# Expert matrices: who makes the first-key one-hot tables

## The chip, the cores and the metric

One Trainium2 chip; the kernel runs on one core of it. The metric is the device time of one execution in microseconds (us). The engines are named as in the profile: PE (TensorE matmuls), PEld (its weight loads), DVE (VectorE), ACT (ScalarE), POOL (GpSimd) and SP (SyncE, which here issues transfers). Each runs its own program in order and meets the others at counting semaphores.

## The reference, cut to what matters

One encoder layer for 1024 tokens of width 1024: token mixing, then a retrieval over 128 x 128 = 16,384 single-neuron experts. Each token has 8 heads; each head picks 16 experts, so a token has 128 picks, and an expert's number is a pair of keys (first, second):

```python
idx = first_key * PEER_KEYS + second_key      # PEER_KEYS = 128
g = softmax(best)                             # 16 weights per head
u = exp_u[idx]
a = gelu(einsum('td,ted->te', x, u)) * g
y = einsum('te,ted->td', a, exp_v[idx])
```

## The kernel before

The part that matters is `up_and_lists` (L1681 to L2181). It treats the eight blocks of 128 tokens in two ways. For the first four (ND = 4, numbered b = 0 to 3) it builds, for each token, a dense 128 x 128 matrix of expert weights, and stores these matrices in HBM (`route_scratch`); for the other four it only makes lists of expert numbers, and their experts' rows are gathered by indirect DMA.

A token's matrix is one matmul, `second` transposed times `first` (L2172). Both operands have one row per pick. A row of `first` is a one-hot of the pick's first key, times its weight; a row of `second` is a one-hot of its second key. They are made 8 tokens at a time (GROUP = 8; 16 groups, q = 0 to 15, to a block) in two slots, s = q % 2:
- DVE, L1993: eight `tensor_scalar` a group, one per token, which compare the key numbers with the token's first keys and multiply by the weights: 128 x 128 f32 each, two operands taken from one column (`key_pair`, `scaled`).
- ACT, L2091: eight activations a group, the distances |key number - second key|, written into `second`. ACT runs two groups ahead.
- DVE, L1999: one compare over the whole slot of `second` turns distances into ones and zeros, and raises `onehots`.
- PE: the eight matmuls, in two halves; each half raises `matrices`. Ahead of them in each group stands one unit (three matmuls) of another product, the up-projection of dense expert chunks (`piece`, L2127).
- ACT, L2109: copies each half out of PSUM into `stage` (`staged`). When a block is done, SP sends `stage` to HBM in 8 transfers of 1 MB (L1792), between loads of the next weights (`sc_u_raw`).

A slot may be written again when the matmuls of the group that used it are done (the waits on `matrices`, L1989 and L2088).

Between these, DVE's own queue holds other work, written out by hand in `tables` (L1979 to L2010). In blocks 0 and 1 each group is followed by one part of the top-16 selection of a later block (`routing`, L1866; parts 5 to 8 are its longest). In blocks 2 and 3 (DOT_BLOCKS) each group holds two dot products of a gathered expert row with the tokens (`pair_dot`, L2012), one ahead of the compare and one behind it. Their rows come through two buffers (`sc_eq` and `sc_prod`): POOL issues an indirect DMA for pick n (`fetch_pair`, L1832) once dot n - 2 has freed the buffer. Before the change POOL does nothing else in these blocks. One subtraction (`split_low`, L2027) follows groups 1 and 9. After the four blocks POOL fetches more rows into a ring of six (L1824), and DVE takes their dots (L2020).

Of the kernel before, what the change touches and what calls it, by code (L numbers as in the profile page):

```python
# [22 lines left out]
ALU = mybir.AluOpType  # L23
# [3 lines left out]
P = 128  # L27
# [18 lines left out]
WEIGHT_SCALE = 2.0 ** 14  # L46

ND = 4
# [11 lines left out]
class Layer:  # L60
# [1620 lines left out]
    def up_and_lists(self, vals, idxs, h2_hi, h2_lo, expert_at, expert_of, weight_of, dots):  # L1681
# [29 lines left out]
        listed = self.sem("sc_listed")  # L1711
        onehots = self.sem("sc_onehots")
        keys_ready = self.sem("sc_keys_ready")
        distances = self.sem("sc_distances")
        matrices = self.sem("sc_matrices")
        staged = self.sem("sc_staged")
# [31 lines left out]
        with ExitStack() as c:  # L1748
# [28 lines left out]
            with nc.Block() as block:  # L1777
# [40 lines left out]
                @block.gpsimd  # L1818
                def _(pool):
                    pool.iota(iota16[:], [[1, TOPK]], base=0, channel_multiplier=0, allow_small_or_imprecise_dtypes=True).then_inc(iotas, 1)  # L1820
                    pool.iota(key_of[:], [[1, KEYS]], base=0, channel_multiplier=0, allow_small_or_imprecise_dtypes=True).then_inc(iotas, 1)
                    every_u = self.u_rows.rearrange("i j d -> (i j) d")

                    def fetch_u(n):  # L1824
                        r = (n - GROUP_DOTS) % U_RING
                        if n >= GROUP_DOTS + U_RING:

                            pool.wait_ge(dotted, n - U_RING + 1)
                        pool.indirect_dma_start(u_rows[r], None, every_u,
                                                bass.IndirectOffsetOnAxis(ap=expert_at[:, n // P, n % P:n % P + 1], axis=0)).then_inc(u_got[r], 16)  # L1830

                    def fetch_pair(n):  # L1832
                        r = n % PAIR
                        if n >= PAIR:

                            pool.wait_ge(dotted, n - PAIR + 1)
                        pool.indirect_dma_start(pair_rows[r], None, every_u,
                                                bass.IndirectOffsetOnAxis(ap=expert_at[:, 0, n:n + 1], axis=0)).then_inc(pair_got[r], 16)
                    pool.wait_ge(listed, 1)
                    for i, b in enumerate(DOT_BLOCKS):  # L1840

                        pool.wait_ge(chosen, TURN_OF[b] + 1)
                        for n in range(i * BLOCK_DOTS, (i + 1) * BLOCK_DOTS):
                            fetch_pair(n)
                    pool.wait_ge(listed, BETWEEN)
                    pool.wait_ge(matrices, ND * QUADS)
                    for n in range(GROUP_DOTS, EARLY_DOTS):
                        if n == GROUP_DOTS + 2:

                            pool.wait_ge(stored, 16 * PIECES * ND)  # L1850
                        fetch_u(n)

                @block.vector
                def _(dve):
# [124 lines left out]
                    def tables(b):  # L1979
                        dve.wait_ge(turned, TURN_OF[b] + 1)  # L1980
                        dve.tensor_copy(key_pair[:].rearrange("k a t -> k (a t)"), ps[:, 4, 0:2 * P]).then_inc(keys_ready, 1)
                        do(dve.tensor_scalar(scaled[:], ps[:, 4, 2 * P:3 * P], WEIGHT_SCALE, None, ALU.mult))
                        all_so_far()
                        dve.wait_ge(keys_ready, b + 1)
                        for q in range(GROUPS):
                            s = q % 2
                            if b or q >= 2:

                                dve.wait_ge(matrices, b * QUADS + 2 * q - 2)  # L1989
                            for i in range(GROUP):  # L1990
                                t = q * GROUP + i
                                at_first = key_pair[:, 0, t:t + 1]
                                dve.tensor_scalar(first[:, s, i], key_of[:], at_first, scaled[:, t:t + 1], ALU.is_equal, ALU.mult)  # L1993

                            if b in DOT_BLOCKS:
                                at = DOT_BLOCKS.index(b) * BLOCK_DOTS + q * PER_GROUP
                                pair_dot(at)
                            dve.wait_ge(distances, b * GROUPS + q + 1)
                            dve.tensor_scalar(second[:, s].rearrange("k g n -> k (g n)"), second[:, s].rearrange("k g n -> k (g n)"),  # L1999
                                              0.0, None, ALU.is_equal).then_inc(onehots, 1)  # L2000
                            if b < BETWEEN:
                                routing(TURN_OF[ND + b], q)
                            if b in DOT_BLOCKS:
                                pair_dot(at + 1)
                            if q == 1:
                                split_low(b * PER_BLOCK + SPLITS + AHEAD - 1)
                            if q == GROUPS // 2 + 1:
                                split_low(b * PER_BLOCK + SPLITS + AHEAD)

                        dve.wait_ge(onehots, (b + 1) * GROUPS)  # L2010
# [114 lines left out]
                @block.tensor  # L2125
                def _(pe):
                    def piece(j, k):  # L2127
                        s, r = j % 2, j % SPLITS
                        if k == 0:

                            pe.wait_ge(u_split, j + 1)
                            if j >= 2:
                                pe.wait_ge(gelu_done, j - 1)
                        part, cols = k // 4, slice((k % 4) * P, (k % 4 + 1) * P)
                        last = self.product3(pe, hid[s], u_hi[r][:, part, cols], u_lo[r][:, part, cols], h2_hi[:, k, 0:HALF], h2_lo[:, k, 0:HALF],
                                             k == 0, k == KT - 1)
                        if k == KT - 1:
                            last.then_inc(hidden, 1)
                    def turn_list(g):
                        pe.wait_ge(chosen, TURN_OF[ND + g] + 1)  # L2140
                        if g >= 2:

                            pe.wait_ge(listed, g - 1)
                        pe.transpose(ps[:, 2 + g % 2, 0:P], picks[:, 0], self.ident[:]).then_inc(turned, 1)
                    for b in range(ND):
                        for i in range(AHEAD):
                            for k in range(KT):
                                piece(b * PER_BLOCK + i, k)
                        pe.wait_ge(chosen, TURN_OF[b] + 1)
                        if b:  # L2150

                            pe.wait_ge(staged, b * QUADS)
                        for i in range(3):
                            last = pe.transpose(ps[:, 4, i * P:(i + 1) * P], picks[:, i], self.ident[:])
                        last.then_inc(turned, 1)
                        for q in range(GROUPS):
                            for unit in range(UNITS * q, UNITS * (q + 1)):
                                piece(b * PER_BLOCK + AHEAD + unit // KT, unit % KT)
                            pe.wait_ge(onehots, b * GROUPS + q + 1)
                            s = q % 2  # L2160
                            for half in range(2):
                                quad = 2 * q + half
                                if quad < 4:

                                    pe.wait_ge(keys_ready, b + 1)
                                if b or quad >= 4:

                                    pe.wait_ge(staged, b * QUADS + quad - 3)
                                for t in range(QUAD):
                                    to = ps[:, 4 + quad % 4, t * KEYS:(t + 1) * KEYS]  # L2170
                                    tok = half * QUAD + t
                                    last = pe.matmul(to, second[:, s, tok], first[:, s, tok], start=True, stop=True)  # L2172
                                last.then_inc(matrices, 1)
                            if q == TURN_AT and b < BETWEEN:
                                turn_list(b)
                    for j in range(LATE, C):
                        for k in range(KT):
                            piece(j, k)
                        for g in range(BETWEEN, NG):
                            if j - LATE == STEPS[g] + TURN_AT // PARTS:  # L2180
                                turn_list(g)  # L2181
# [461 lines left out]
```

## Time and profile before

| | |
|---|---|
| three runs | 4506.31, 4509.48, 4510.59 us (median 4509.48) |
| the profiled execution | 4506.8 us, of which 4505.2 us from its first to its last instruction |
| the four blocks (tables, with what lies between) | about 2123 to 2625 us of it |
| busy, whole span | PE 3661.2, DVE 2892.1, ACT 1518.0, POOL 1260.1 us |

How to read the rows: times are microseconds from the first instruction. In a timeline a row is start, duration, engine, line, operation, tiles and shapes, a count where equal instructions are merged, and in brackets how long the engine had been idle and who ended that. "Idle" means without an instruction in execution; a wait is put down to the semaphore that came last.

### The profile page before, as it was taken

The page shows a single profiled execution, that of the slowest core. Times are in us where ns is not written, and L with a number is a line of the kernel's source. Part 1 is how long each engine was busy: PE and PEld are TensorE (multiplying, and loading weights), DVE is VectorE, ACT ScalarE, POOL GpSimd, SP SyncE. Part 2 cuts the span into 40 slices and gives each one's busy share as a digit, 9 for nine tenths or more (in the row PEclk, how much of TensorE's full clock was granted, in tenths as well). Part 3 has the DMA queues.
Part 4 walks back from the last instruction along what each step waited for, and adds up shares of the span by engine and source line. Part 5 has one row for each costly group of instructions (what it writes and reads, how often), then busy time and mean ns, then how long its engine had stood idle before and what let it go on. Part 6 is the DMA issues. An engine that isn't in the chain of part 4 may idle for free. (4 is left out here: it accounts for less than half of the span.)

```text
span 4505.2 us, 49138 instructions
## 1 busy us (share of the span) xinstructions
PE 3661.2 (81%) x17580; PEld 2759.8 (61%) x17580; DVE 2892.1 (64%) x5556; ACT 1518.0 (34%) x2202; POOL 1260.1 (28%) x1072
## 2 busy tenths in 40 slices
PE   1899999979568976896675654599999999999895
PEld 1677777767457765785564443366566666665553
DVE  5666666631531256796787758677777777776565
ACT  3444444434433433213676531122122222221211
POOL 0000000000100000000002237577667767665442
PEclk8999999989679987997897877799999999999998
DMA  3111111129148885102435788899999999999996
GB/s 138 36 52 47 50 50 52 54 96 323 61 151 297 300 332 193 61 23 94 126 113 182 229 257 302 325 399 406 377 397 406 401 388 398 406 396 372 358 362 245
DMA packets 384570, 1042.20 MB, mean 231 GB/s; under 512 B 33392, under 2 KB 102384, under 8 KB 381168
## 3 DMA queue, kind: packets, MB, share of 16 engines
q0 software_dynamic: 152352, 563.15, 33.0%
q1 hardware_dynamic: 179808, 334.33, 22.0%
q10 hardware_dynamic: 52208, 142.10, 8.2%
q8 instruction: 118, 1.93, 0.2%
q14 instruction: 84, 0.69, 0.0%
HBM read 897.37 MB, written 142.08 MB: 231 GB/s over the span
## 5 line engine op out<-in xcount | busy, mean ns | idle before, releaser
L2322 POOL DMA_INDIRECT ex_v_rows<-peer_v_dram,expert_of x512 | 634.0, 1238 | 296.0 <-PE psum L2551 148.3
L2454 DVE TENSOR_TENSOR y<-y,psum 128x512 f32<-128x512 f32 x512 | 349.9, 683 | 382.2 <-PE psum L397 379.7
L395 PE MATMUL psum<-h_hi 128*128 128x512 f32 x1024 | 422.0, 412 | 66.4 <-ACT sc_gelu_t L2071 52.3
L2447 DVE CUSTOM_DVE_ANT_1 ex_u_rows<-ex_u_rows,y 128x1024 f32<-128x1024 f32 x352 | 429.7, 1221 | 57.5 <-DMA ex_u_rows<-u_rows_scratch,expert_at 41.6
L2314 POOL DMA_INDIRECT ex_u_rows<-u_rows_scratch,expert_at x352 | 382.9, 1088 | 271.8 <-DVE dots L2447 178.3
L395 PE MATMUL psum<-h_hi,v_hi 128*128 128x512 f32 x1024 | 430.0, 420 | 1.4 <-issue 0.8
L396 PE MATMUL psum<-h_lo,h_hi 128*128 128x512 f32 x1024 | 407.8, 398 | 0.0
L397 PE MATMUL psum<-h_hi,h_lo 128*128 128x512 f32 x1024 | 406.2, 397 | 0.0
L396 PE MATMUL psum<-h_lo,v_hi 128*128 128x512 f32 x1024 | 405.4, 396 | 0.0
L397 PE MATMUL psum<-h_hi,v_lo 128*128 128x512 f32 x1024 | 404.4, 395 | 0.0
L2551 PE MATMUL psum<-ex_v_rows,ex_spread 128*32 128x512 f32 x2048 | 284.8, 629 | 96.6 <-DMA ex_v_rows<-peer_v_dram,expert_of 95.9
L1147 POOL TENSOR_TENSOR sp_sg<-sp_sg,sp_u 128x1024 f32<-128x1024 f32 x8 | 20.6, 2572 | 1214.4 <-DVE sp_sg L1207 1214.4
L395 PE MATMUL psum<-in_hi,att_w_hi_t 128*128 128x512 f32 x768 | 316.3, 412 | 36.8 <-DVE att_w_lo_t L848 35.0
L395 PEld LDWEIGHTS psum<-h_hi,v_hi 128*128 128x128 f32 x1024 | 194.6, 190 | 224.3 <-issue 130.5
L2172 PE MATMUL psum<-sc_first,sc_second 128*128 128x128 f32 x1024 | 173.4, 339 | 167.7 <-DVE sc_second L1999 167.6
L2365 ACT ACTIVATE h_hi<-g 128x512 fp32r<-128x512 f32 x128 | 80.8, 631 | 679.0 <-DVE g L2477 434.0
L397 PE MATMUL psum<-in_hi,att_w_lo_t 128*128 128x512 f32 x768 | 302.3, 394 | 0.0
L396 PE MATMUL psum<-in_lo,att_w_hi_t 128*128 128x512 f32 x768 | 301.4, 392 | 0.0
L395 PEld LDWEIGHTS psum<-h_hi 128*128 128x128 f32 x1024 | 198.5, 194 | 144.5 <-issue 93.0
L2172 PEld LDWEIGHTS psum<-sc_first,sc_second 128*128 128x128 f32 x1024 | 159.5, 245 | 198.7 <-DVE sc_second L1999 198.6
L397 PEld LDWEIGHTS psum<-h_hi,h_lo 128*128 128x128 f32 x1024 | 197.3, 193 | 43.5
L397 PEld LDWEIGHTS psum<-h_hi,v_lo 128*128 128x128 f32 x1024 | 195.1, 191 | 44.2
(380 smaller groups left out, 7853.2 us busy)
## 6 DMA issues: line engine op xcount, KB each, us to landing
y<-peer_v_dram SPq DMA_DIRECT2D x128, 512.0 KB, 8.4
route_scratch<-sc_stage SPq DMA_DIRECT2D x32, 1024.0 KB, 10.3
g<-route_scratch SPq DMA_DIRECT2D x128, 256.0 KB, 6.2
att_raw<-w_in_dram SPq DMA_DIRECT2D x48, 512.0 KB, 3.6
sc_u_raw<-peer_uT_dram SPq DMA_DIRECT2D x48, 512.0 KB, 6.4
front_r_in<-peer_uT_dram SPq DMA_DIRECT2D x40, 512.0 KB, 4.8
u_rows_scratch<-front_r_out ACTq DMA_DIRECT2D x40, 512.0 KB, 5.1
y<-peer_uT_dram ACTq DMA_DIRECT2D x40, 512.0 KB
```

Of the source, the lines that this page charges most:

```text
L395: pe.matmul(out, w_hi, x_hi, start=start, stop=False)
L396: pe.matmul(out, w_hi, x_lo, start=False, stop=False)
L397: return pe.matmul(out, w_lo, x_hi, start=False, stop=stop)
L1147: pool.tensor_tensor(sg[:, j % 2], sg[:, j % 2], u[:, j % 2], ALU.mult).then_inc(gated, 1)
L2172: last = pe.matmul(to, second[:, s, tok], first[:, s, tok], start=True, stop=True)
L2314: pool.indirect_dma_start(u_rows[:, r], None, every_u, bass.IndirectOffsetOnAxis(ap=expert_at[:, n // P, n % P:n % P + 1], axis=0)).then_i ...
L2322: pool.indirect_dma_start(v_rows[:, r * LANES + lane], None, every_v, bass.IndirectOffsetOnAxis(ap=expert_of[:, m // 32, t:t + 1], axis=0) ...
L2365: act.activation(act_hi[ring], g[:, s], ACT.Copy).then_inc(a_hi_done, 1)
L2447: dve.tensor_tensor_reduce(out=halves(u_rows[:, r]), in0=halves(u_rows[:, r]), in1=rows, scale=1.0, scalar=0.0, op0=ALU.mult, op1=ALU.add, ...
L2454: dve.tensor_tensor(to, to, ps[:, n % 4], ALU.add).then_inc(added, 1)
L2551: last = pe.matmul(ps[lane * 32:(lane + 1) * 32, 4 + half], spread[:, first:first + 32], v_rows[:, r * LANES + lane, half * HALF:(half + 1 ...
```

## The change

The eight tables of a group are issued by POOL instead of DVE, with the same operands (`first_tables`). They get a semaphore of their own, `firsts`, for which PE waits beside `onehots`; a further one, `weights_ready`, tells POOL that `scaled` is written. POOL takes over the wait on `matrices` that frees a slot, and runs one group ahead: it makes the tables of groups 0 and 1 at the start, then in each group q those of group q + 1. In blocks 2 and 3 the two row fetches of group q + 1 stand in POOL's queue behind the tables of group q + 1. DVE keeps the compare, the dots, the routing and the subtractions.

```diff
+        weights_ready = self.sem("sc_weights_ready")
+        firsts = self.sem("sc_firsts")
...
-                    pool.wait_ge(listed, 1)
-                    for i, b in enumerate(DOT_BLOCKS):
-
-                        pool.wait_ge(chosen, TURN_OF[b] + 1)
-                        for n in range(i * BLOCK_DOTS, (i + 1) * BLOCK_DOTS):
-                            fetch_pair(n)
+                    def first_tables(b, q):
+                        s = q % 2
+                        if b or q >= 2:
+
+                            pool.wait_ge(matrices, b * QUADS + 2 * q - 2)
+                        for i in range(GROUP):
+                            t = q * GROUP + i
+                            last = pool.tensor_scalar(first[:, s, i], key_of[:], key_pair[:, 0, t:t + 1], scaled[:, t:t + 1], ALU.is_equal, ALU.mult)
+                        last.then_inc(firsts, 1)
+                    pool.wait_ge(iotas, 2)
+                    for b in range(ND):
+                        if b in DOT_BLOCKS:
+                            at = DOT_BLOCKS.index(b) * BLOCK_DOTS
+                            pool.wait_ge(listed, 1)
+
+                            pool.wait_ge(chosen, TURN_OF[b] + 1)
+                            for n in range(at, at + PER_GROUP):
+                                fetch_pair(n)
+                        pool.wait_ge(keys_ready, b + 1)
+                        pool.wait_ge(weights_ready, b + 1)
+                        first_tables(b, 0)
+                        for q in range(GROUPS):
+                            if q + 1 < GROUPS:
+                                first_tables(b, q + 1)
+                                if b in DOT_BLOCKS:
+                                    for n in range(at + (q + 1) * PER_GROUP, at + (q + 2) * PER_GROUP):
+                                        fetch_pair(n)
...
-                        do(dve.tensor_scalar(scaled[:], ps[:, 4, 2 * P:3 * P], WEIGHT_SCALE, None, ALU.mult))
-                        all_so_far()
-                        dve.wait_ge(keys_ready, b + 1)
+                        dve.tensor_scalar(scaled[:], ps[:, 4, 2 * P:3 * P], WEIGHT_SCALE, None, ALU.mult).then_inc(weights_ready, 1)
                         for q in range(GROUPS):
                             s = q % 2
-                            if b or q >= 2:
-
-                                dve.wait_ge(matrices, b * QUADS + 2 * q - 2)
-                            for i in range(GROUP):
-                                t = q * GROUP + i
-                                at_first = key_pair[:, 0, t:t + 1]
-                                dve.tensor_scalar(first[:, s, i], key_of[:], at_first, scaled[:, t:t + 1], ALU.is_equal, ALU.mult)
-
                             if b in DOT_BLOCKS:
...
                             pe.wait_ge(onehots, b * GROUPS + q + 1)
+                            pe.wait_ge(firsts, b * GROUPS + q + 1)
...
                                     pe.wait_ge(keys_ready, b + 1)
+                                    pe.wait_ge(weights_ready, b + 1)
```

## Rows read from the trace of the kernel before

**Rows 1.** Busy time by stretch: ten groups of blocks 0 and 1, then others.
```profile
core 0: us, PE busy (x) PEld busy (x) DVE busy (x) ACT busy (x) POOL busy (x), PEclk, DMA share, GB/s
2126.39:2178.73 52.34, 33.63 (x188) 29.01 (x189) 51.62 (x193) 45.42 (x105) 0.00 (x0) 0.83 0.07 20
2251.10:2303.37 52.27, 34.30 (x190) 29.23 (x190) 51.55 (x194) 46.07 (x107) 0.00 (x0) 0.82 0.07 19
2178.73:2198.07 19.34, 15.02 (x99) 12.50 (x97) 14.06 (x48) 19.34 (x50) 0.00 (x0) 0.94 0.05 18
...
2364.50:2476.00 111.50, 62.92 (x309) 53.65 (x310) 86.06 (x222) 71.28 (x164) 32.52 (x30) 0.72 0.59 184
...
2202.50:2241.30 38.80, 33.21 (x143) 26.71 (x142) 26.58 (x79) 12.61 (x15) 0.00 (x0) 0.93 0.98 289
```

**Rows 2.** Timeline of DVE: compares of groups 0, 10, 15 (block 0) and 0, 15 (block 2).
```profile
2126.39 0.69 DVE L1999 TENSOR_SCALAR sc_second<-sc_second 128x1024 f32<-128x1024 f32 x1
...
2178.73 0.69 DVE L1999 TENSOR_SCALAR sc_second<-sc_second 128x1024 f32<-128x1024 f32 x1
...
2198.07 0.69 DVE L1999 TENSOR_SCALAR sc_second<-sc_second 128x1024 f32<-128x1024 f32 x1 [1.10 <-ACT sc_second L2091]
...
2377.79 0.69 DVE L1999 TENSOR_SCALAR sc_second<-sc_second 128x1024 f32<-128x1024 f32 x1 [9.31 <-ACT sc_second L2091]
...
2471.71 0.69 DVE L1999 TENSOR_SCALAR sc_second<-sc_second 128x1024 f32<-128x1024 f32 x1
```

**Rows 3.** Timelines of DVE and ACT, one late group of block 0.
```profile
2182.48 2.13 DVE L1993 TENSOR_SCALAR sc_first<-sc_key_of,sc_key_pair,sc_scaled 128x128 f32<-128x128 f32 x8
2185.95 0.69 DVE L1999 TENSOR_SCALAR sc_second<-sc_second 128x1024 f32<-128x1024 f32 x1 [1.34 <-ACT sc_second L2091]
...
2183.50 2.42 ACT L2091 ACTIVATE sc_second<-sc_key_of,sc_key_pair 128x128 f32<-128x128 f32 x8
2185.80 1.94 ACT L2109 ACTIVATE sc_stage<-psum 128x512 f32<-128x512 f32 x2
2187.53 2.42 ACT L2091 ACTIVATE sc_second<-sc_key_of,sc_key_pair 128x128 f32<-128x128 f32 x8
```

**Rows 4.** Timelines of DVE and POOL, one group of block 2.
```profile
2452.43 1.23 DVE L2017 CUSTOM_DVE_ANT_0 sc_eq<-sc_eq,sc_rows_first 128x1024 f32<-128x1024 f32 x1 [0.85 <-DMA sc_eq<-u_rows_scratch,expert_at]
...
2453.58 0.69 DVE L1999 TENSOR_SCALAR sc_second<-sc_second 128x1024 f32<-128x1024 f32 x1
2455.01 1.23 DVE L2017 CUSTOM_DVE_ANT_0 sc_prod<-sc_prod,sc_rows_first 128x1024 f32<-128x1024 f32 x1 [0.74 <-DMA sc_prod<-u_rows_scratch,expert_at]
...
2456.16 2.17 DVE L1993 TENSOR_SCALAR sc_first<-sc_key_of,sc_key_pair,sc_scaled 128x128 f32<-128x128 f32 x8
2458.51 1.22 DVE L2017 CUSTOM_DVE_ANT_0 sc_eq<-sc_eq,sc_rows_first 128x1024 f32<-128x1024 f32 x1 [0.18 <-DMA sc_eq<-u_rows_scratch,expert_at]
...
2453.93 1.15 POOL L1837 DMA_INDIRECT sc_eq<-u_rows_scratch,expert_at  x1 [3.23 <-DVE dots L2017]
2456.51 0.94 POOL L1837 DMA_INDIRECT sc_prod<-u_rows_scratch,expert_at  x1 [1.43 <-DVE dots L2017]
```

**Rows 5.** The tile `sc_eq`: its transfers, from issue to landing.
```profile
DMA to landing us min/median/max: 4.3/4.5/8.4
```

**Rows 6.** POOL's other instructions; the last row is ns min/median/max.
```profile
L1821 POOL IOTA sc_key_of<- 128x128 f32 x1 | 0.2, 233 | 0.0
...
L2637 POOL MEMSET const-float32-0.0<- 128x1 f32 x1 | 0.1, 98 | 0.4 <-issue 0.4
...
L1147 POOL TENSOR_TENSOR sp_sg<-sp_sg,sp_u x8: 2352/2367/3220, 1185.5 to 1232.4; 128x1024 f32<-128x1024 f32 x8
```

**Rows 7.** Fetches on POOL under DVE work, and all fetches into `sc_prod`.
```profile
2385.20 1.22 DVE L2031 TENSOR_TENSOR h_lo<-sc_u_raw,h_hi 128x1024 fp32r<-128x1024 f32 x1
...
2385.56 1.68 POOL L1837 DMA_INDIRECT sc_prod<-u_rows_scratch,expert_at  x1 [1.29 <-DVE dots L2017]
...
2672.36 1.23 DVE L2025 CUSTOM_DVE_ANT_0 sc_stage<-sc_stage,sc_rows_first 128x1024 f32<-128x1024 f32 x1 [1.02 <-DMA sc_stage<-u_rows_scratch,expert_at]
...
2672.44 1.95 POOL L1829 DMA_INDIRECT sc_first<-u_rows_scratch,expert_at  x1 [0.30 <-issue]
...
L1837 POOL DMA_INDIRECT sc_prod<-u_rows_scratch,expert_at x32: 933/938/1680, 2360.7 to 2617.3; - x32
```

**Rows 8.** Groups by line: two of the routing's instructions, which read two tiles.
```profile
L1883 DVE TENSOR_TENSOR sc_eq<-sc_pos_h,sc_iota 128x2048 f16<-128x2048 f16 x12 | 27.5, 2289 | 0.3
...
L1887 DVE TENSOR_TENSOR sc_prod<-sc_eq,top_idxs 128x2048 f16<-128x2048 f16 x12 | 14.7, 1228 | 0.1
```

## The prediction

> **What bounds the kernel now.** I read three views. First the busy time by stretch: it shows that the four blocks of tables are not bound by one thing. In the first ten groups of blocks 0 and 1, DVE is busy 51.62 of 52.34 us and 51.55 of 52.27, ACT 45.42 and 46.07; in the last five groups of block 0 ACT is busy all 19.34 us [rows 1]. So DVE sets the pace where it carries routing, ACT afterwards. Second the timelines: a late group of block 0 shows DVE's compare idle 1.34 us until ACT's distances, and ACT's period is 2187.53 - 2183.50 = 4.03 us [rows 3]. A group of block 2 shows something else: both dots wait for their rows' transfers (0.85 and 0.74 us), and the fetches for dots [rows 4]. Third the tile view, for the time a fetch takes to land: 4.5 us [rows 5]. The loop in blocks 2 and 3 is then: a dot of 1.15 us (2452.43 to 2453.58), 0.35 until its fetch is issued, 4.58 until the next dot in this buffer starts: 6.08 us [rows 4]. Over 15 groups of block 2 the mean is (2471.71 - 2377.79)/15 = 6.26 us [rows 2]; block 3 repeats it. DVE's work lies inside this loop and does not set it. Between blocks the DMA engines are busy 98% of the time [rows 1], with a store that starts only when a block's last group is staged; so that stretch keeps its length, and what a block gains or loses reaches the end of the kernel.
>
> **What is removed.** Eight tables a group leave DVE: 2.13 us [rows 3], 64 times, 136 us of DVE time. Its worth is not that. In blocks 0 and 1 the gain ends where ACT becomes the bound: at most ACT's idle time in the ten DVE-bound groups, 52.34 - 45.42 = 6.92 and 52.27 - 46.07 = 6.20, together 13.1 us. The late groups gain nothing (ACT). In blocks 2 and 3 the 2.17 us of tables lie while the transfers fly [rows 4]; their removal gives nothing. DVE's dropped waits and the new `weights_ready` replace each other: nothing, hidden under ACT's first two groups of distances.
>
> **What is added: the price of one table on POOL.** No row shows it. The nearest row is the iota over the same 128 x 128 f32: 0.233 us, which reads nothing; that is the lower end. A two-tile operation over 1024 columns took 2.367 us, a one-column memset 0.098 [rows 6]: per column (2367 - 98)/1024 = 2.22 ns, so 128 columns and the start cost 0.38 us; with two more one-column accesses for the key and the weight at 0.10 each, 0.58 us: the upper end. I take the iota with those two accesses, 0.233 + 0.20 = 0.43 us, because a table reads one tile and not two. A group is 8 x 0.43 = 3.44 us (1.86 to 4.64).
>
> The Trainium skill (GPSIMD Engine Reference, Engine selection) advises VectorE for elementwise work and puts GpSimd about 2x slower for two inputs, near line rate for one. By 2x on DVE's 2.13 us a group would be an estimated 4.3 us and the sum below about +60 us.
>
> **What is added: the port.** A fetch takes 0.94 us on POOL (median 938 ns), but 1.68 under DVE's two-input subtraction, 1.95 under a dot [rows 7], and 1.15 where it starts under the compare [rows 4]. So POOL's work stops while such a DVE instruction runs, and I expect the tables to stop too. The other way round a DVE instruction may wait for one table, at most 0.58 us; DVE has 2.1 us a group to spare, so this costs nothing.
>
> The Trainium skill says the same as a rule (SBUF — State Buffer, Who interferes with whom): the second SBUF port pair is an exclusive lock, and a VectorE instruction with two SBUF inputs shuts out a GpSimd one that reads SBUF. For the fetches the trace agrees (0.94 against 1.68 and 1.95 us); for tables no row shows it.
>
> **What is moved.** In blocks 2 and 3 the two fetches of a group now stand behind eight tables in POOL's queue, and the tables behind the second fetch, which waits for the second dot. Behind POOL's wait on `matrices` stand the tables and both fetches, and for these wait DVE's dots, the compare between them, and PE. POOL's work for a group is in one queue: tables 3.44, fetches 1.15 + 0.94, two gaps of 0.30 (2.69 for both fetches) [rows 4, 7]: 6.13 us without collisions, as long as the loop of 6.26. DVE holds the port for two dots and a compare, 2 x 1.22 + 0.69 = 3.1 us of every group. The first dot starts 4.5 us after its fetch, right among the tables: I count 1.22 us for it. The compare and the second dot fall mostly beside the fetches, whose 1.15 has part of it: I count nothing, and 1.9 more as the bound. That gives 7.35 us a group, 1.1 more than 6.26. Over 2 x 15 groups: +33 us (bounds: 0 without collisions, +89 with all).
>
> In blocks 0 and 1 POOL needs 3.44 + 0.69 = 4.13 us a group under one compare, as long as ACT's 4.03. In the routing groups 5 to 8 DVE holds the port longer: two compares of 2.29 and two products of 1.23 [rows 8] are 7.0 us a block. Of the 13.1 us to be won these two blocks lose about 9, since POOL is only one group ahead: -4 us (bounds: -13 and 0).
>
> **The sum.** +33 - 4 = +29 us on the profiled 4506.8 us: 4536. The median of the runs is 2.7 us above that execution: 4539 us. A measurement of this kernel can tell a change from none beyond about 0.2%, 9 us.
>
> **The rivals.**
> - *POOL becomes the bound in all four blocks.* If a table costs 0.58 us, a group's tables are 4.64; blocks 0 and 1 then run at 4.64 + 0.69 = 5.33 us instead of (2198.07 - 2126.39)/15 = 4.78 [rows 2], +8 each and up to +16 with the routing's collisions; blocks 2 and 3 at 4.64 + 2.69 + 1.22 = 8.55, +69, or +126 with all collisions. Together +85 to +158: 4594 to 4668 us. For it: two operands from single columns and two operations, which neither the iota nor the product has. Against: a table reads one tile.
> - *The tables hide and the loop stays* (faster). If a table costs under 0.29 us, POOL's group in blocks 2 and 3 is 2.3 + 2.69 + 1.22 = 6.2 us, no longer than the loop; they stay, and blocks 0 and 1 give up to 13.1 us: 4496 to 4500. For it: the iota's 0.233 us. Against: it reads nothing. The place is POOL's queue between two fetches; 0.29 us is the point from which it decides.
> - *Both cancel.* Between 0.29 and 0.36 us a table, the 5 to 13 us won in blocks 0 and 1 and what blocks 2 and 3 lose differ by less than 9 us: 4500 to 4518.
>
> **How the numbers follow.** Chances: forecast (0.36 to 0.58 us a table) 0.46, 4518 to 4594; POOL bound everywhere 0.20; cancel 0.18; hide 0.16. So slower 0.66, same 0.18, faster 0.16. The range goes down to the hiding case, 4497 us. Above, it takes in the forecast's case and the lower half of the dear tables, to 4625.
>
> **What would show it.** In the profile after: the tables on POOL with a median near 0.43 us, longer where a dot runs; compares in blocks 2 and 3 about 7.4 us apart instead of 6.26; dots that wait for transfers, and transfers issued late after tables rather than 0.35 us behind a dot; PE waiting for POOL in the routing groups; blocks 0 and 1 shorter by a few us; ACT's copies waiting longer in blocks 2 and 3. The prediction is wrong if a table costs far from 0.43 us, if tables don't stop under dots, or if the fetches land faster when they leave in pairs.

## The result and the profile after

The changed kernel takes 4726.66 us (median of 4 runs, 4722.93 to 4734.24), the kernel before 4509.09 (4 runs, 4506.31 to 4510.59). The ratio is 1.0484, interval 1.0468 to 1.0499: 218 us slower. The forecast of 4539 us had the direction right and the size wrong: the time lies 102 us above the end of its range. It also had part of the place wrong: 78 of the 218 us are lost in and right behind blocks 0 and 1, where it had a gain of 4. The profiled execution has a span of 4725.1 us.

The first row to read is that of the tables, in the costliest groups of the page after (busy us and mean ns of one behind the bar, then the idle time before them); the second is the same line's own view (ns min/median/max):
```profile
L1848 POOL TENSOR_SCALAR sc_first<-sc_key_of,sc_key_pair,sc_scaled 128x128 f32<-128x128 f32 x512 | 500.9, 989 | 98.3 <-DVE sc_key_pair L2004 50.3
...
L1848 POOL TENSOR_SCALAR sc_first<-sc_key_of,sc_key_pair,sc_scaled x512: 780/787/4514, 2131.1 to 2840.0; 128x128 f32<-128x128 f32 x171
```
A table costs 0.787 us at the median. The forecast took 0.43, and its upper bound was 0.58. Eight tables started one behind the other take 8 x 0.774 = 6.2 us, where DVE made them in 2.13 [rows 3].

Busy time by stretch, after: blocks 0 to 3, each from its first compare to its last (columns as in [rows 1]).
```profile
2133.18:2240.41 107.23, 57.96 (x275) 48.97 (x276) 38.64 (x121) 66.39 (x153) 107.23 (x120) 0.72 0.04 13
2300.36:2400.65 100.29, 57.61 (x275) 49.43 (x276) 38.98 (x121) 66.24 (x153) 100.29 (x111) 0.75 0.04 14
2462.94:2627.55 164.61, 69.54 (x285) 60.47 (x285) 48.53 (x76) 66.20 (x152) 153.04 (x143) 0.66 0.33 104
2683.86:2846.49 162.63, 72.54 (x285) 62.34 (x285) 48.37 (x78) 66.16 (x152) 151.79 (x144) 0.64 0.33 105
```
In blocks 0 and 1 POOL is busy for all 107.23 and all 100.29 us; DVE, which set the pace in most groups there before, is busy 36 and 39% of the time. In blocks 2 and 3 POOL is busy 93%; two gaps in front of the fetches fill most of the rest. From the first compare to the last, the same stretches took 71.7, 70.6, 93.9 and 92.4 us before (blocks 0 and 2: [rows 2]): +35.5, +29.7, +70.7 and +70.2 (blocks 1 and 3 of before stand in the next fence). From the last compare of one block to the first of the next it was 53.0, 56.0 and 56.3 us and is 60.0, 62.3 and 56.3: +7, +6 and 0. Together about +219, all of the 217.6 us that the medians differ by. (Of the two profiled executions the one after is 6.8 us later ahead of block 0 and 6.1 us shorter behind block 3; these stretches also differ by several us between runs that leave them as they are.)
```profile
2251.10:2321.74 70.64, 48.17 (x286) 40.71 (x286) 65.50 (x241) 64.44 (x154) 0.00 (x0) 0.87 0.07 20
2528.03:2620.45 92.42, 57.70 (x285) 49.01 (x285) 78.90 (x196) 65.49 (x152) 31.57 (x29) 0.78 0.59 177
```

One group of block 2, DVE's dots and compares (answer to [rows 4]):
```profile
2526.04 1.22 DVE L2030 CUSTOM_DVE_ANT_0 sc_eq<-sc_eq,sc_rows_first 128x1024 f32<-128x1024 f32 x1 [7.65 <-DMA sc_eq<-u_rows_scratch,expert_at]
...
2527.19 0.69 DVE L2012 TENSOR_SCALAR sc_second<-sc_second 128x1024 f32<-128x1024 f32 x1
2528.22 1.22 DVE L2030 CUSTOM_DVE_ANT_0 sc_prod<-sc_prod,sc_rows_first 128x1024 f32<-128x1024 f32 x1 [0.34 <-DMA sc_prod<-u_rows_scratch,expert_at]
...
2536.99 1.23 DVE L2030 CUSTOM_DVE_ANT_0 sc_eq<-sc_eq,sc_rows_first 128x1024 f32<-128x1024 f32 x1 [7.55 <-DMA sc_eq<-u_rows_scratch,expert_at]
...
2538.14 0.69 DVE L2012 TENSOR_SCALAR sc_second<-sc_second 128x1024 f32<-128x1024 f32 x1
```
The same group on POOL:
```profile
2523.83 0.80 POOL L1848 TENSOR_SCALAR sc_first<-sc_key_of,sc_key_pair,sc_scaled 128x128 f32<-128x128 f32 x1
...
2526.18 2.27 POOL L1848 TENSOR_SCALAR sc_first<-sc_key_of,sc_key_pair,sc_scaled 128x128 f32<-128x128 f32 x1
...
2528.44 1.66 POOL L1848 TENSOR_SCALAR sc_first<-sc_key_of,sc_key_pair,sc_scaled 128x128 f32<-128x128 f32 x1
...
2532.59 1.01 POOL L1839 DMA_INDIRECT sc_eq<-u_rows_scratch,expert_at  x1 [0.17 <-issue]
...
2533.90 0.95 POOL L1839 DMA_INDIRECT sc_prod<-u_rows_scratch,expert_at  x1 [0.30 <-issue]
```
The compares are 2538.14 - 2527.19 = 10.95 us apart; they were 6.26. The dot waits 7.65 us for its rows, which DVE's waits name as the transfer. This transfer isn't slower: it still lands in 4.4 us at the median (first row of the next fence, as [rows 5]). It is issued late, behind eight tables. The transfer into `sc_prod` leaves 1.3 us behind it, where it was 2.6, and does land later: 5.3 us (second row; 4.6 before). But over blocks 2 and 3 DVE waits only 10.4 us for that one. And the table that runs beside the first dot and the compare takes 2.27 us, the one beside the second dot 1.66. The group adds up as POOL's queue: 6.2 of tables, 2.4 of their stalls, 1.01 + 0.95 of fetches, 0.17 + 0.30 of gaps: 11.0.
```profile
DMA to landing us min/median/max: 4.2/4.4/7.7
...
DMA to landing us min/median/max: 5.0/5.3/8.5
```

### The profile page after: what moved, and what is told of

Its sections match the earlier page's. It is cut to its first block and busy times, and to the rows that moved or that the text cites. A ratio compares the mean times of both kernels' runs of the same rounds, so it can differ in the third digit from the quotient of the medians.

```text
span 4725.1 us, 49150 instructions
## 1 busy us (share of the span) xinstructions
PE 3727.2 (79%) x17580; PEld 2819.3 (60%) x17580; DVE 2769.5 (59%) x5044; ACT 1522.5 (32%) x2202; POOL 1753.5 (37%) x1584
## 5 line engine op out<-in xcount | busy, mean ns | idle before, releaser
L1848 POOL TENSOR_SCALAR sc_first<-sc_key_of,sc_key_pair,sc_scaled 128x128 f32<-128x128 f32 x512 | 500.9, 989 | 98.3 <-DVE sc_key_pair L2004 50.3
L2187 PE MATMUL psum<-sc_first,sc_second 128*128 128x128 f32 x1024 | 215.1, 395 | 336.7 <-DVE sc_second L2012 254.1
L2187 PEld LDWEIGHTS psum<-sc_first,sc_second 128*128 128x128 f32 x1024 | 199.5, 299 | 371.5 <-DVE sc_second L2012 284.7
```

The source lines that it names most:

```text
L1848: last = pool.tensor_scalar(first[:, s, i], key_of[:], key_pair[:, 0, t:t + 1], scaled[:, t:t + 1], ALU.is_equal, ALU.mult)
```

## The experiments

Three theories stood against each other. A: the price of a table, paid in POOL's queue in all four blocks. B: the order of that queue in blocks 2 and 3, fetches behind tables. C: collisions with DVE's dots, as a part beside A. Ratios are to the kernel before, run beside each.

| run | us (median) | ratio (interval) | blocks 0 to 3, us |
|---|---|---|---|
| the change | 4726.66 | 1.0484 (1.0468 to 1.0499) | 107.2, 100.3, 164.6, 162.6 |
| e2_first_two_blocks | 4586.71 | 1.0171 (1.0148 to 1.0194) | 106.3, 100.1, 92.9, 92.9 |
| e3_last_two_blocks | 4651.27 | 1.0314 (1.0290 to 1.0338) | 71.9, 71.5, 163.9, 162.8 |
| e5_add_mult | 4576.99 | 1.0161 (1.0141 to 1.0182) | 73.1, 69.8, 127.4, 125.6 |
| e6_no_dots | 4683.98 | 1.0380 (1.0358 to 1.0402) | 106.2, 101.5, 138.0, 137.5 |
| e7_add_mult_no_dots | 4527.86 | 1.0043 (1.0026 to 1.0059) | 74.4, 72.5, 104.5, 103.7 |
| e8_fetch_between | 4701.23 | 1.0427 (1.0409 to 1.0445) | 107.7, 100.8, 150.3, 146.1 |
| e4_half_each | 4504.71 | 0.9989 (0.9976 to 1.0001) | 69.2, 68.1, 94.3, 94.8 |
| e10_half_again | 4503.54 | 0.9986 (0.9973 to 0.9999) | 70.4, 67.8, 93.9, 93.1 |
| e9_three | 4502.60 | 0.9986 (0.9974 to 0.9997) | 68.0, 67.4, 92.7, 93.4 |

**e1_prices: what one table costs, and which part of it.** The kernel before, with a stretch of POOL instructions alone at its start. Its time, 4587.68 us in one run, is of no use beyond that: the stretch comes on top.
```diff
+ pool.tensor_scalar(out[:, i], keys[:, 0:P], vals[:, i:i+1], vals[:, i+8:i+9], ALU.is_equal, ALU.mult)  # the table
+ pool.tensor_scalar(out[:, i], keys[:, 0:P], 3.0, 2.0, ALU.is_equal, ALU.mult)
+ pool.tensor_scalar(out[:, i], keys[:, 0:P], vals[:, i:i+1], None, ALU.is_equal)
+ pool.tensor_scalar(out[:, i], keys[:, 0:P], 3.0, None, ALU.is_equal)
+ pool.tensor_scalar(out[:, i], keys[:, 0:P], vals[:, i:i+1], vals[:, i+8:i+9], ALU.add, ALU.mult)
+ pool.tensor_scalar(out[:, i], keys[:, 0:P], 3.0, None, ALU.mult)
...
+ pool.tensor_tensor(out[:, i], keys[:, 0:P], vals[:], ALU.mult)
```


> The kernel before, with a stretch of POOL instructions alone ahead of it, in which no other engine works; the rest is unchanged. It prices a table part by part. A table took 0.787 us on POOL where no DVE work overlapped it. Theory 1, cost by column: (0.787 - 0.098)/128 = 5.4 ns a column, so 16 columns about 0.18 us, 512 columns 2.9, 1024 columns 5.6, and operands from single columns or immediates cost the same. Theory 2, cost at the start (the two operands from single columns, the start of the instruction): 16 columns about 0.5 us or more, 1024 columns under 3 us, and the form with two immediates well below the table, near the iota's 0.233. Theory 3, the compare is dear: add and mult with the same operands cost less than is_equal and mult. A two-tile product over 128 columns: 0.38 us by the row of 1024 columns.

Each line's own view (ns min/median/max, then first and last start), in the order of the diff, the table over 16, 512 and 1024 columns ahead of the product:
```profile
L182 POOL TENSOR_SCALAR probe_out<-probe_keys,probe_vals x8: 780/781/805, 2.3 to 7.8; 128x128 f32<-128x128 f32 x8
L185 POOL TENSOR_SCALAR probe_out<-probe_keys x8: 640/644/645, 8.6 to 12.9; 128x128 f32<-128x128 f32 x8
L188 POOL TENSOR_SCALAR probe_out<-probe_keys,probe_vals x8: 601/602/604, 13.6 to 17.7; 128x128 f32<-128x128 f32 x8
L191 POOL TENSOR_SCALAR probe_out<-probe_keys x8: 526/527/528, 18.4 to 21.8; 128x128 f32<-128x128 f32 x8
L194 POOL TENSOR_SCALAR probe_out<-probe_keys,probe_vals x8: 441/447/448, 22.5 to 25.5; 128x128 f32<-128x128 f32 x8
L197 POOL TENSOR_SCALAR probe_out<-probe_keys x8: 523/524/544, 26.0 to 29.5; 128x128 f32<-128x128 f32 x8
L200 POOL TENSOR_SCALAR probe_out<-probe_keys,probe_vals x8: 423/426/433, 30.1 to 32.9; 128x16 f32<-128x16 f32 x8
L203 POOL TENSOR_SCALAR probe_out<-probe_keys,probe_vals x4: 2071/2072/2072, 33.4 to 39.6; 128x512 f32<-128x512 f32 x4
L206 POOL TENSOR_SCALAR probe_out<-probe_keys,probe_vals x4: 3777/3777/3778, 41.8 to 53.0; 128x1024 f32<-128x1024 f32 x4
L212 POOL TENSOR_TENSOR probe_out<-probe_keys,probe_vals x8: 447/448/453, 58.9 to 61.8; 128x128 f32<-128x128 f32 x8
```
Alone, with DVE idle, the table costs 0.781 us, as in the stage: the median there is no contention. From 512 to 1024 columns it grows by (3.777 - 2.072)/512 = 3.33 ns a column; 128 of these are 0.43 us, and 0.35 to 0.37 remain as a start. With an addition in place of the comparison the same instruction costs 0.447: in this form the comparison costs 0.33 us more. Whether the comparison is slow or the pair of addition and product quick is not told by that: a single product with a constant takes 0.524, as much as a single comparison (0.527). The two operands from single columns cost 0.781 - 0.644 = 0.14. That the price goes by columns alone falls (0.426 us at 16 columns); a start of its own holds in part; the dear comparison holds.

**e2_first_two_blocks and e3_last_two_blocks: where it is lost.** POOL makes the tables of two blocks only, DVE those of the others.
```diff
+ ON_POOL = (8, 8, 0, 0)     # e3: (0, 0, 8, 8)
- for i in range(GROUP):
+ for i in range(ON_POOL[b]):
      ...
+ for i in range(ON_POOL[b], GROUP):
+     dve.tensor_scalar(first[:, s, i], key_of[:], key_pair[:, 0, t:t + 1], scaled[:, t:t + 1], ALU.is_equal, ALU.mult)
- pe.wait_ge(firsts, b * GROUPS + q + 1)
+ if ON_POOL[b]:
+     ...
```


> Tables on POOL in blocks 0 and 1 only; in blocks 2 and 3 on DVE as before, fetches as before. Theory A, the price of a table: POOL bounds these two blocks at 8 x 0.77 us and more a group, and they lose what they lost in the changed kernel: 35.5 + 29.6 us in the tables and 7 + 6 behind the last compare, +78 us, about 4587. Theory B, the fetches queued behind tables are what costs: no fetch is touched here, so 4496 to 4509.

> Tables on POOL in blocks 2 and 3 only; in blocks 0 and 1 on DVE as before. Theory A (price, with collisions under the dots): +71 and +69 us in the tables, about +140: 4650. Theory B (fetches behind tables alone): the whole loss, +218: 4727. The compares of block 2 should be 10.9 us apart by both.

Both times are those of A (4587 and 4650). 1.0171 and 1.0314: the two excesses sum to 0.0485, the change's is 0.0484, and in each run the blocks that DVE keeps have about their length of before. So the two parts simply add. Blocks 0 and 1 have no fetches, and lose 77 us all the same; so B can't be the cause there.

**e5_add_mult: only the comparison taken out.** The tables hold the sum of two keys, times the weight, so the matrices have no meaning; every instruction, wait and place in the queue stays.
```diff
- ..., ALU.is_equal, ALU.mult)
+ ..., ALU.add, ALU.mult)
```


> The changed kernel with add and mult in the tables on POOL instead of is_equal and mult; the tables hold other numbers, so the matrices mean nothing. Alone such an instruction takes 0.447 us (0.44 from start to start) against the table's 0.781, which is the price that the prediction had set (0.43). Theory A: only the price was wrong. Then this kernel behaves as the prediction was worked out: compares in blocks 2 and 3 about 7.4 us apart, +33 us there, -4 in blocks 0 and 1: about 4539, with the second dot's and the compare's collisions as a bound up to 4595. Theory B (the order of the queue, with fetches behind tables, is what costs most): 4650 or more, since the order is the same.

Groups by line of e5, the row of the tables:
```profile
L1848 POOL TENSOR_SCALAR sc_first<-sc_key_of,sc_key_pair,sc_scaled 128x128 f32<-128x128 f32 x512 | 326.5, 653 | 109.5 <-DVE sc_key_pair L2004 50.0 <-DVE sc_scaled L2005 46.1 <-PE psum L2187 12.5
```
Blocks 0 and 2 of e5, busy time by stretch:
```profile
2129.07:2202.19 73.12, 48.59 (x286) 41.47 (x286) 38.82 (x120) 64.48 (x154) 71.80 (x124) 0.86 0.06 20
...
2380.53:2507.93 127.40, 63.68 (x285) 56.07 (x285) 52.32 (x76) 65.90 (x152) 111.35 (x141) 0.70 0.41 130
```
This tests the forecast at about its own price: a table alone takes 0.447 us, where it took 0.43. The time, 4576.99 us, is above A's 4539 and under its bound of 4595; B's 4650 is missed by far. The excess falls from 0.0484 to 0.0161: 0.0323, about 146 of the 218 us, hang on having a comparison there and not an addition. Blocks 0 and 1 together come out at 142.9 us against 142.3 before. Blocks 2 and 3 still lose 33 us each, twice the forecast's 33 for both: there the change is slower at the forecast's price too.

**e6_no_dots and e7_add_mult_no_dots: what the dots' collisions cost.** The 64 dots of blocks 2 and 3 are left out, so the numbers that they feed are missing; their transfers, waits and counts stay. e7 has the addition of e5 as well.
```diff
- dve.tensor_tensor_reduce(out=pair_rows[r], in0=pair_rows[r], in1=rows[0], ...).then_inc(dotted, 1)
+ dve.tensor_scalar(dots[:, 0, n:n + 1], pair_rows[r][:, 0:1], 1.0, None, ALU.mult).then_inc(dotted, 1)
```


> The changed kernel without the 64 dots of blocks 2 and 3 (a one-column product stands in each one's place, with the same waits; their results are left out). Theory C, DVE's two-input instructions stop the tables: without them POOL needs 8 x 0.774 + 2.45 + 0.3 to 0.6 = 9.0 to 9.2 us a group instead of 10.9, about -56 us: 4671. If the dots did not stop the tables: no change, 4727.

> Both edits together (add and mult in the tables, dots of blocks 2 and 3 left out). POOL's group is 8 x 0.44 + 2.45 + 0.3 to 0.6 = 6.3 to 6.6 us, little more than the 6.26 of before; blocks 0 and 1 a few us less: 4500 to 4520. The difference to the kernel with dots and the same tables is the price of the collisions at the price that the prediction had set: by the prediction 1.22 us a group, about 37 us.

Block 2 of e6, busy time by stretch:
```profile
2468.64:2606.61 137.97, 68.84 (x285) 59.10 (x285) 17.36 (x47) 66.03 (x152) 127.25 (x144) 0.65 0.39 122
```
Block 2 of e7:
```profile
2390.61:2495.07 104.46, 56.77 (x285) 48.99 (x285) 20.00 (x48) 64.32 (x152) 83.62 (x141) 0.75 0.49 155
```
POOL's waits in blocks 2 and 3 of e7 (us in total, times, longest):
```profile
POOL sc_first L1850 <- PE psum L2188: 20.9, 14, 2.7
```
Both kernels came out slower than expected, e6 by 13 us and e7 by 8. At the price with the comparison the dots are worth 0.0484 - 0.0380 = 0.0104 (47 us), at the price with the addition 0.0161 - 0.0043 = 0.0118 (53 us): 1.6 to 1.8 us in each of 30 groups. This is C, and it is the smaller part. Without dots and comparison the loop of block 2 takes 104.46/15 = 7.0 us, not 6.26, though POOL is busy only 80% of it. Part of the rest is the wait above, 20.9 us in both blocks: POOL waits for PE to have used the buffer of two groups ago. What the remainder of these 0.0043 is made of, no run settles.

**e8_fetch_between: the order of the queue.** Four tables, a fetch, four tables, a fetch, in place of eight tables and two fetches.
```diff
      last = pool.tensor_scalar(first[:, s, i], ...)
+     if fetch is not None and i == GROUP // 2 - 1:
+         fetch_pair(fetch)
  last.then_inc(firsts, 1)
+ if fetch is not None:
+     fetch_pair(fetch + 1)
```


> The changed kernel with another order in POOL's queue in blocks 2 and 3: four tables, one fetch, four tables, one fetch. Theory A (POOL's queue is full: price, fetches, collisions): the same work in the same queue, 4715 to 4735. Theory B (fetches late behind tables): dots get their rows earlier and the loop comes back toward 6.26 us, so much less, down to about 4590.

A dot of block 2 and the fetch that runs beside it, timelines of DVE and POOL of e8:
```profile
2529.04 1.23 DVE L2031 CUSTOM_DVE_ANT_0 sc_eq<-sc_eq,sc_rows_first 128x1024 f32<-128x1024 f32 x1 [4.12 <-DMA sc_eq<-u_rows_scratch,expert_at]
...
2529.13 2.02 POOL L1839 DMA_INDIRECT sc_prod<-u_rows_scratch,expert_at  x1 [0.17 <-issue]
```
B falls: the order is worth about 25 us, and 193 stay. But A's range is missed as well, by 14 us: the order isn't worth nothing. Here a dot meets a fetch, which it stretches from 0.94 to 2.02 us, instead of a table; the tables' mean in blocks 2 and 3 falls from 1.064 to 0.883 us, and the groups of blocks 2 and 3 come 10.0 and 9.7 us apart on average (150.3/15 and 146.1/15) instead of 11.0 and 10.8.

**e4_half_each, e10_half_again and e9_three: what can be won.** POOL makes four tables of each group in blocks 0 and 1 (e4, and e10, which is e4 once more) or three (e9), DVE the others; blocks 2 and 3 are as before.
```diff
+ ON_POOL = (4, 4, 0, 0)     # e9: (3, 3, 0, 0)
```


> Blocks 0 and 1: four tables of a group on POOL and four on DVE; blocks 2 and 3 as before. Theory A (price): POOL needs 4 x 0.77 + 0.69 = 3.8 us a group, under ACT's 4.03; DVE gives up 1.07 us a group, so the ten DVE-bound groups of each block shorten until ACT is the bound: up to 13 us less, about 4497 to 4503. If collisions with the routing keep POOL behind in groups 5 to 8: 4505 to 4512. Theory B says no loss either, so this run tells whether the gain that was counted (13 us at most) is there.

> As the kernel with four tables of a group on POOL and four on DVE in blocks 0 and 1, with three on POOL and five on DVE. Theory A: POOL needs 3 x 0.77 + 0.69 = 3.0 us a group and is no longer late in the routing groups; DVE keeps 0.27 us a group more. A few us under the kernel before, as with four: 4498 to 4508. If the late groups 5 to 9 come from POOL's collisions, the ten routing groups take less than with four (53.0 and 51.9 us by the windows of that run); if from DVE's own routing, as long or longer.

> The kernel with four tables of a group on POOL and four on DVE in blocks 0 and 1 once more, for its interval: 0.9976 to 1.0001 of before. Theory A: the block lengths fell by 2.4 and 2.5 us, so about 5 us less than before, 0.999. No gain at all: 1.000.

Blocks 0 and 1 of e4, busy time by stretch:
```profile
2129.68:2198.93 69.25, 47.81 (x286) 40.43 (x286) 53.09 (x181) 64.22 (x154) 64.75 (x62) 0.86 0.07 20
2251.55:2319.65 68.10, 47.08 (x286) 40.14 (x286) 53.29 (x180) 64.16 (x154) 59.00 (x56) 0.88 0.07 20
```
DVE's busy time in block 0 falls from 65.68 to 53.09 us, but the block only from 71.7 to 69.2, with ACT at 64.22: of the at most 13.1 us that the forecast had for both blocks, about 5 are won. All three runs lie 0.11 to 0.14% below the kernel before, two of them with an interval just below 1. By these ratios the gain is 5 to 6 us, barely clear of none, and these are the fastest versions found. From the first compare to the twelfth (the window of the expectation), blocks 0 and 1 take 53.0 and 51.9 us in e4, 54.2 and 51.6 in e10, 51.8 and 51.2 in e9. With three tables on POOL they are shorter in both blocks, as POOL's collisions would have it, but e4 and its repetition differ by as much as 1.1 us themselves.

## Why the prediction was wrong, by its own steps

**What bounds the kernel, and what the removal is worth: right, with a size to mend.** Blocks 0 and 1 gave less than the bound (e4: 5 of 13 us). That the removal is worth nothing in blocks 2 and 3 isn't shown by itself: every run that takes the tables from DVE there gives them to POOL, and the lightest of these, e7, is still slower there than the kernel before (104.5 against 93.9 us).

**The price of one table: the step that failed.** "0.233 + 0.20 = 0.43 us" should have been 0.78, and the upper bound of 0.58 lay below that too. Both were built from rows of an iota, a memset and a product [rows 6]; none of them compares. e1 shows what that leaves out: with an addition the table costs 0.447 us, within 4% of 0.43, and with the comparison 0.33 more. That 0.43 comes so near 0.447 is luck: by its parts (0.233, and 0.10 for each operand from a column) a product with a constant would cost less than 0.43, and it took 0.524. The point for the POOL-bound rival, 0.58 us, was passed, and that rival is what happened: POOL bound in all four blocks. It had 0.20, and its time, 4594 to 4668 us, is too low by the same 0.2 us a table. With 0.774 its sums are 6.19 + 0.69 = 6.9 us a group in blocks 0 and 1 (measured 107.23/15 = 7.1 and 100.29/15 = 6.7) and 6.19 + 2.69 + 1.22 = 10.1 in blocks 2 and 3 (measured 11.0).

The Trainium skill (GPSIMD Engine Reference, Engine selection) speaks for VectorE, and was right in that. Its factor isn't borne out: 0.774 us against DVE's 2.13/8 = 0.27 is 2.9 times, not about 2 and not line rate, and the estimated +60 us by it compares with 218 measured.

**The port: right; its count: too low.** Tables do stop beside dots: 0.787 us alone, 1.66 beside a dot, 2.27 beside a dot and the compare. The forecast counted only the first dot, 1.22 us a group, since the second would fall beside the fetches. It doesn't: the two fetches leave 1.3 us apart behind the tables and land 4.4 and 5.3 us later (medians), among the next group's tables, so both dots fall there. The stalls are 2.4 us in the group shown, and leaving the dots out gives back 1.6 to 1.8. The Trainium skill (SBUF — State Buffer, Who interferes with whom) has it as an exclusive lock. For tables this was open in the forecast; now the trace agrees: the two tables are longer by 1.48 and 0.87 us, where the dots last 1.22 and the compare 0.69.

**The other way round: not quite free.** DVE waits for POOL too: the compare, 0.69 us alone, takes up to 0.88. With POOL as the bound this costs nothing that shows.

**What is moved: right.** Dots wait for transfers issued late, 222.6 us for `sc_eq` in blocks 2 and 3 (10.1 us before), with the landing time of these unchanged. ACT's copies wait for PE 191.5 us there (56.3 before), as the forecast named. Waits from the first compare of block 2 to the last of block 3 (us in total, times, longest):
```profile
DVE sc_eq L2030 <- DMA sc_eq<-u_rows_scratch,expert_at: 222.6, 31, 8.3
...
ACT sc_stage L2122 <- PE psum L2187: 191.5, 62, 8.3
```

**Blocks 0 and 1, -4 us: wrong through the price, and not far off without it.** At 0.447 us a table (e5) they take 0.6 us more than before, too little to be called a loss or a gain.

**Between blocks, no change: wrong by 13 us.** The last compare of block 0 starts at 2240.41 us, but the last table ends at 2224.51 + 21.89 = 2246.40, and PE's products of that group start 0.10 us behind it. POOL's and PE's timelines there, then the busy time in the stretch of these products, after and (last row) before:
```profile
2224.51 21.89 POOL L1848 TENSOR_SCALAR sc_first<-sc_key_of,sc_key_pair,sc_scaled 128x128 f32<-128x128 f32 x26
...
2246.50 3.75 PE L2187 MATMUL psum<-sc_first,sc_second 128*128 128x128 f32 x16 [4.26 <-issue]
...
2246.50:2250.25 3.75, 3.75 (x17) 3.75 (x18) 0.00 (x0) 1.04 (x1) 0.00 (x0) 0.50 0.00 0
...
2198.82:2200.87 2.05, 2.05 (x17) 2.05 (x18) 1.98 (x12) 1.91 (x3) 0.00 (x0) 1.00 0.00 0
```
PE starts 6.09 us after that compare instead of 0.75 (2198.82 - 2198.07 before). It had been idle for 4.26 us, and in its 16 products the granted clock was 0.50 (1.2 GHz), where the same products had 1.00 (2.4 GHz) before: they take 3.75 us instead of 2.05. +5.3 + 1.7 = +7.0, as the stretch measured. Block 1 ends alike: its last table ends at 2406.64 us, and PE starts at 2406.74, 6.09 us after the compare. In block 2 the last tables end at 2613.30 + 8.40 = 2621.70 us, ahead of the last compare at 2627.55, which waited for its dot; there PE follows the compare by 0.75 us as before, and nothing is added.

**The sum.** Of 218 us, 146 are the price of the comparison over an addition, 53 the dots' collisions at the price with the addition (counted: 37), and 19 what is left, the rest of the queue among it (counted, with the gain of blocks 0 and 1: -8). At the price that was taken, e5 is 1.0161, about 4582 us: outside the 4539, but inside the forecast's own case of 4518 to 4594.

## What to carry to other kernels

Before work moves to another engine, measure one instruction of exactly that form there, alone: here the comparison made it cost 1.7 times what it cost with an addition, and no row of other operations showed it. Then add up the receiving engine's whole queue for a period, gaps and stalls included; if it also issues transfers, work placed ahead of them delays everything that waits for their data, even where the transfers themselves are no slower. Ask last what the relieved engine was worth: here ACT stood close behind, and relief of 12.6 us of DVE's time in a block bought 2.5.

## What the runs showed of the hardware that was not expected

- On POOL the operation in an instruction of the same shape decides its price: 0.781 us with `is_equal` and `mult`, 0.447 with `add` and `mult`, over the same 128 x 128 f32 and the same two operands (e1). With the comparison it is a start of 0.35 to 0.37 us and 3.33 ns a column.
- One operation with a constant, a comparison (0.527 us) or a product (0.524), costs more than an addition and a product with two operands from columns (0.447). So the forms can't be ranked by their number of operations or operands.
- What waits for POOL can pay a second time on PE: over block 0 PE's granted clock was 0.72 instead of 0.86, and in the block's last products, which PE began after 4.26 us without work, it was 0.50 (1.2 GHz) instead of 1.00 (2.4 GHz): 3.75 us instead of 2.05.
- Of two indirect fetches issued 1.3 us apart, the second lands later: 5.2 to 5.3 us at the median in the five runs that issue them so (the change, e3, e5, e6, e7), 4.5 to 4.8 in the four where 2.5 us or more lie between them (before, e2, e4, e8). No run tells why.
